# RWKV's LoRA products, key norm and first pair of heads moved between the layer's first weight fills, mixed tiles rounded one by one, and the feed-forward output's wait split by part

## The reference

```python
h = _rms(x) * norm1_g
proj = h @ w_in            # aq, ak, av | rw: r, k, v, wd, ad, gd | rq, rk, rv, rg | three gates
# RWKV-7 on rw: z = h + shift_mu * (h_prev - h), over 14 tiles of 128 columns
w_log = -softplus(-(w0 + tanh(wd) @ w2)) - 0.5 ; a = sigmoid(a0 + ad @ a2) ; g = sigmoid(gd) @ g2
kk = k * k_k ; kk = kk / max(norm over the head of kk, 1e-12) ; k = k * (1 + (a - 1) * k_a)
# then a scan over positions for 8 heads of 64 (here 4 pairs), bonus = sum(r * k * r_k) * v
mixed = g0 * (attention @ w_attn_o) + g1 * (rwkv @ w_rwkv_o) + g2 * (retention @ w_ret_o)
x = x + mixed @ w_out
h2 = _rms(x) * norm2_g
x = x + (silu(h2 @ w_ffn_gate) * (h2 @ w_ffn_up)) @ w_ffn_down
```

## Time and profile before

| | |
|---|---|
| time, median of 3 runs | 3206.34 us (3206.17 to 3213.61) |
| the profiled execution | 3204.21 us, of it 3202.4 us span |
| PE busy in the span | 97% |
| mean granted TensorE clock | 0.989 |
| DVE, ACT, POOL busy | 36%, 34%, 45% |

### The profile page before, as it was taken

How to read it: one execution, slowest core, us unless ns; L and a number is a source line. 1 busy time by engine, 2 the same in 40 slices (tenths; PEclk the granted TensorE clock), 3 DMA queues, 4 the chain that set the end, 5 groups by cost and what they waited for, 6 DMA issues and landing times.

```text
span 3202.4 us, 52487 instructions
## 1 busy us (share of the span) xinstructions
PE 3103.2 (97%) x20754; PEld 2474.5 (77%) x20754; DVE 1140.3 (36%) x1645; ACT 1100.8 (34%) x1547; POOL 1431.9 (45%) x1824
## 2 busy tenths in 40 slices
PE   8998989999999999999999999999999999899999
PEld 6887778868878777887777888787688877688877
DVE  3025532361110456232556322226533156542210
ACT  4444543342222433113443322222411245432222
POOL 3542244635555454223335555556322242565555
PEclk9999899999999999999999999999999999999999
DMA  5223332213223232114323222233221242422223
GB/s 219 98 99 119 119 113 82 96 53 105 98 92 105 79 108 99 61 61 161 110 89 139 97 93 98 94 110 118 82 77 62 100 159 73 151 99 94 96 98 125
DMA packets 102130, 330.89 MB, mean 103 GB/s; under 512 B 10064, under 2 KB 10448, under 8 KB 101200
## 3 DMA queue, kind: packets, MB, share of 16 engines
q1 hardware_dynamic: 75088, 272.87, 25.0%
q10 hardware_dynamic: 26880, 55.65, 4.8%
HBM read 299.64 MB, written 28.84 MB: 103 GB/s over the span
## 4 chain that ended last, share of the span: by engine, by line
issue 40%; POOL 31%; PE 25%; DVE 1%; DMA 1%; ACT 1%; POOLq 0%; DVEq 0%; SPq 0%; ACTq 0%
POOL w_lo L317 31%; PE psum L346 20%; PE psum L682 4%; DMA H<-scratch 0%; DMA arena<-in_w_ada 0%; DVEq L1507 0%; POOLq L313 0%; PE psum L878 0%; PE psum L899 0%; POOLq L323 0%; DVE HL L1510 0%; PE psum L901 0%; PE psum L858 0%; DVE arena L2100 0%; PE psum L895 0%
## 5 line engine op out<-in xcount | busy, mean ns | idle before, releaser
L317 POOL TENSOR_TENSOR w_lo<-w_raw,w_hi 128x256 fp32r<-128x256 f32 x1820 | 1431.7, 819 | 1766.2 <-ACT w_hi L932 1567.8
L346 PE MATMUL psum<-XH,w_hi 128*128 128x512 f32 x2592 | 1052.2, 406 | 9.6 <-DVE XL L1510 3.5
L346 PE MATMUL psum<-XH,w_lo 128*128 128x512 f32 x2592 | 1014.5, 391 | 0.0
L346 PE MATMUL psum<-XL,w_hi 128*128 128x512 f32 x2592 | 1014.2, 391 | 0.0
L932 ACT ACTIVATE w_hi<-w_raw 128x1024 fp32r<-128x1024 f32 x436 | 460.3, 1056 | 807.5 <-PE psum L346 699.5
L346 PEld LDWEIGHTS psum<-XH,w_hi 128*128 128x128 f32 x2592 | 489.0, 189 | 145.1 <-issue 27.0
L346 PEld LDWEIGHTS psum<-XL,w_hi 128*128 128x128 f32 x2592 | 488.8, 189 | 105.1
L346 PEld LDWEIGHTS psum<-XH,w_lo 128*128 128x128 f32 x2592 | 489.6, 189 | 101.1 <-issue 7.7
L346 PE MATMUL psum<-HH,w_hi 128*128 128x512 f32 x976 | 391.3, 401 | 27.6 <-DVE HL L1510 20.7
L346 PE MATMUL psum<-HL,w_hi 128*128 128x512 f32 x976 | 385.5, 395 | 0.0
L346 PE MATMUL psum<-HH,w_lo 128*128 128x512 f32 x976 | 385.4, 395 | 0.0
(11 more groups left out here) (328 smaller groups left out, 2378.3 us busy)
## 6 DMA issues: line engine op xcount, KB each, us to landing
w_raw<-in_fills SPq DMA_DIRECT2D x488, 512.0 KB, 3.2
scratch<-arena ACTq DMA_DIRECT2D x86, 256.0 KB, 2.0
arena<-scratch ACTq DMA_DIRECT2D x10, 1024.0 KB, 7.8
arena<-in_w_ada SPq DMA_DIRECT2D x4, 2048.0 KB, 19.4
H<-scratch ACTq DMA_DIRECT2D x4, 2048.0 KB, 14.9
scratch<-H SPq DMA_DIRECT2D x2, 2048.0 KB, 8.3
arena<-scratch ACTq DMA_DIRECT2D x2, 2048.0 KB, 9.0
arena<-scratch ACTq DMA_DIRECT2D x2, 1792.0 KB, 19.7
```

Of the source, the lines that this page charges most:

```text
L317: ins = nc.gpsimd.tensor_tensor(w_lo[:, to:to + FILL // 4], w_raw[:, of:of + FILL // 4], w_hi[:, to:to + FILL // 4].bitcast(F32), ALU.subt ...
L346: ins = mm(out_ap, wt[:, w:w + 128], xt[:, x0:x0 + T], start=first and k == 0 and o == 0, stop=last and k == n - 1 and o == 2)
```

## The change

In each hybrid layer:

- The z fills come in another order (`Z_ORDER`): the tiles of wd, ad and gd first, then k, r, the two attention tiles, v. SP loads them one by one in that order. They are `z_fill(q)`, written out, no longer a loop from q = 4 to 11.
- Of RWKV's preparation, the three groups of LoRA products stand behind z fills 5, 7 and 9, the sums of squares of k behind z fill 11 (PE). ACT evaluates and takes out accordingly, between its roundings of weights; it does the key norm's Ln and Exp ahead of rounding behind z fill 12. DVE does the running sum of pair 0 at z fill 9, its key (`key(0)`) at 12 and its operands (`operands(0)`) at 13, ahead of the subtractions into XL. The shift comes with its own fill.
- Between the first mid fill and the scan there are now four bonus products with 13 mid blocks behind each (60 blocks in PREP instead of 80); SCAN has 172 instead of 152, three at each of its steps, and 3 or 2 instead of 4 or 3 at its last six.
- Attention's and retention's outputs are rounded and subtracted tile by tile, two of them before ACT's and DVE's last work on retention, and `gemm512`'s first half fill waits tile by tile.
- Gate A is fetched before retention's output is rounded, and waited for alone; gate C comes next, H last, with a wait of its own.
- Each mixed tile is rounded as soon as it is summed, between the roundings of weights, and DVE subtracts the one before.
- `gemm2816` (all three layers) waits for the first 16 tiles at its first block and for the last six at its third part (blocks 17 to 22).

```diff
-R_KB, U_KB = 92, 44
+R_KB, U_KB = 94, (68, 70, 72, 74, 101, 103, 105, 107)
+
+Z_ORDER = [14, 15, 6, 7, 8, 9, 2, 3, 4, 5, 0, 1, 10, 11, 12, 13]
...
-PREP = [8, 8, 8, 6, 6] + 4 * [11]
-SCAN = [2 + k % 2 for k in range(SLOTS * NCH // 2)] + [4, 4, 4, 4, 3, 3]
+PREP = [8] + 4 * [13]
+SCAN = [3] * (SLOTS * NCH // 2) + [3, 3, 3, 3, 2, 2]
...
@@ -623,15 +630,41 @@
-                gemm_rms(f0, c0, 8, 24 * l, 2 * l, l)
+                gemm_rms(f0, c0, 0, 24 * l, 2 * l, l)
...
+                def z_fill(q):
+
+                    j = q % 4
+                    pe.wait_ge(lo_ready, f0 + q + 1)
+                    pe.wait_ge(chunk_out[j], c0 + q // 4 + l * SKEW[j])
...
+                        if q == 15 and k < DT - 1:
...
+
+                def lora(of, rows, x, out):
+
+                    for n in range(4):
+                        if out:
+                            pe.wait_ge(sem("rw_lev"), 12 * l + 4 * out - 4 + n + 1)
+                        mm(bank(4 + n), A(88, 128, of + 128 * n)[rows], A(x)[rows], start=True, stop=True).then_inc(sem("rw_lora"), 1)
+
+                for q in range(4, 16):
+                    z_fill(q)
+                    if q == 5:
+                        pe.wait_ge(sem("rw_act"), 2 * l + 1)
+                        pe.wait_ge(sem("lora_in"), 16 * l + 16)
+                        lora(0, slice(0, 64), 40, 0)
+                    elif q == 7:
+                        lora(0, slice(64, 128), 40, 1)
+                    elif q == 9:
+                        lora(512, slice(0, 128), 42, 2)
+                    elif q == 11:
+                        pe.wait_ge(sem("rw_act"), 2 * l + 2)
+                        for p in range(PAIRS):
+                            ins = mm(bank(4 + p), C("blk1", 128), rp("rn", T, p * T), start=True, stop=True)
+                        ins.then_inc(sem("rp_ss"), 1)
 
...
+                    mm(bank(4 + p), C("blk1", 128), rp("rk", T, (p + 1) % 2 * T), start=True, stop=True).then_inc(sem("rp_bn"), 1)
+                    fill(PREP[1 + p])
...
@@ -1252,19 +1264,60 @@
+                act.preload_act_table(ACT.Sigmoid)
...
+                z_hi = lambda q: hi(f0 + q // 4 * 4, q % 4)
+                act.wait_ge(sem("rw_mix"), 14 * l + 2)
+                fn(A(40)[0:64], A(40)[0:64], ACT.Tanh)
+                fn(A(42), A(42), ACT.Sigmoid).then_inc(sem("rw_act"), 1)
...
+                    for n in range(4):
+                        act.wait_ge(sem("rw_lora"), 12 * l + first + n + 1)
+                        bias = {"bias": P2(l, name, n)} if name else {}
+                        fn(A(kb, T, n * T), bank(4 + n), func, **bias).then_inc(sem("rw_lev"), 1)
...
+                z_hi(4)
+                z_hi(5)
+                lora_out(76, 0, ACT.Sigmoid, "w0")
+                z_hi(6)
+                z_hi(7)
+                lora_out(44, 4, ACT.Sigmoid, "a0")
+                z_hi(8)
+                z_hi(9)
+                ln_exp_tables()
+                lora_out(52, 8, ACT.Copy)
+                z_hi(10)
+                act.wait_ge(sem("rw_mix"), 14 * l + 6)
+                for p in range(PAIRS):
+                    ins = fn(rp("rn", T, p * T), A(24, T, p * T), ACT.Square, scale=P2(l, "k_k", p))
+                ins.then_inc(sem("rw_act"), 1)
+                decays(0)
+                z_hi(11)
+                act.wait_ge(sem("rp_mx"), l + 1)
+                fn(rp("rn", 4 * T), rp("rn", 4 * T), ACT.Ln)
+                nc.scalar.drain()
+                fn(rp("rn", 4 * T), rp("rn", 4 * T), ACT.Exp, scale=-0.5).then_inc(sem("rp_rn"), 1)
+                z_hi(12)
+                z_hi(13)
+                z_hi(14)
...
+                    fn(XH[:, t * T:(t + 1) * T], A(U_KB[t]), ACT.Copy).then_inc(sem("rms_hi"), 1)
+                z_hi(15)
...
                 dve.wait_ge(sem("rms_rstd"), 2 * l + 1)
                 for q in range(4):
                     take(q, q, f0 + q + 1)
+                    shift(Z_ORDER[q] - 2, q)
...
+                for q in range(4, 12):
+                    take(q, q % 4, f0 + q + 1)
+                    normed(q - 4)
+                    shift(Z_ORDER[q] - 2, q % 4)
+                    if q == 9:
+                        sums(0)
...
+                def key(p):
...
+                def operands(p):
...
+                dve.wait_ge(sem("rp_ss"), l + 1)
+                ts(rp("rn", 4 * T), bank(4, 4 * T), 1e-24, None, ALU.max).then_inc(sem("rp_mx"), 1)
+                for q in range(12, 15):
+                    take(q, q % 4, f0 + q + 1)
+                    shift(Z_ORDER[q] - 2, q % 4)
+                    if q == 12:
+                        key(0)
+                    elif q == 13:
+                        operands(0)
+                for t in range(DT):
+                    dve.wait_ge(sem("rms_hi"), 24 * l + 8 + t + 1)
+                    s = slice(t * T, (t + 1) * T)
+                    lo(XL[:, s], A(U_KB[t]), XH[:, s]).then_inc(sem("rms_x"), 1)
+                take(15, 3, f0 + 16)
+                shift(Z_ORDER[15] - 2, 3)
+
+                drain()
+                for p in range(1, PAIRS):
+                    sums(p)
+                    key(p)
+                    operands(p)
+                    bonus(p - 1)
                 bonus(PAIRS - 1)
...
-                entries(first, f0 + 16, ADA_LATER)
+                entries(first, f0, ADA_LATER)
+                for n, e in enumerate(Z_ORDER):
+                    sp.wait_ge(lo_ready, f0 + n - 1)
+                    sp.dma_start(w_raw[:, n % 2 * FILL:(n % 2 + 1) * FILL], dram["fills"][f0 + ADA_LATER + e])\
+                        .then_inc(w_loaded[n % 2], 16)
...
+
+            def gemm512(f, c, tile0, skew, fills=range(4), ready=None):
...
-                        blocks(j, HH, HL, bank(b), range(4 * h, 4 * h + 4), range(tile0, tile0 + 4), True, True)\
-                            .then_inc(fill_done if h else half_done, 1)
+                        blocks(j, HH, HL, bank(b), range(4 * h, 4 * h + 4), range(tile0, tile0 + 4), True, True,
+                               None if j or h else ready).then_inc(fill_done if h else half_done, 1)
...
-                        if j == 0:
-                            pe.wait_ge(sem("ffn_lo"), value)
+                        if part != 1:
+                            pe.wait_ge(sem("ffn_lo"), value - (FT - 16 if part == 0 else 0))
...
-                pe.wait_ge(sem("at_y"), 2 * l + 1)
-                gemm512(f0 + 64, c0 + 17, 0, l + 1)
-                pe.wait_ge(sem("at_y"), 2 * l + 2)
-                gemm512(f0 + 68, c0 + 19, 4, l + 1)
+                gemm512(f0 + 64, c0 + 17, 0, l + 1, ready=lambda k: pe.wait_ge(sem("at_y"), 8 * l + k + 1))
+                gemm512(f0 + 68, c0 + 19, 4, l + 1, ready=lambda k: pe.wait_ge(sem("at_y"), 8 * l + 4 + k + 1))
...
+                    if p == PAIRS - 1:
+                        mixed(0, at("q", T))
+                        mixed(1, at("q", T, T))
...
+                def mixed(t, y):
+
+                    fn(HH[:, t * T:(t + 1) * T], y, ACT.Copy).then_inc(sem("at_yh"), 1)
...
-                fn(HH[:, 0:4 * T], A(AT["q"], 4 * T), ACT.Copy).then_inc(sem("at_yh"), 1)
                 act.preload_act_table(ACT.Sigmoid)
                 act.wait_ge(sem("rt_done"), l * PAIRS + PAIRS)
                 for k in range(MID - 5, MID - 1):
                     act.wait_ge(spilled[k % 4], spill_done(l, k))
-                fn(HH[:, 4 * T:8 * T], A(RQ, 4 * T), ACT.Copy).then_inc(sem("at_yh"), 1)
-                from_scratch(A(76, 8 * T), GATE_A, 8, "gate_a_h_in")
-                from_scratch(H[:], H_TILE, 8, "gate_a_h_in")
+                from_scratch(A(76, 8 * T), GATE_A, 8, "gate_a_in")
+                for t in range(4):
+                    mixed(4 + t, A(RQ, T, t * T))
                 takes(ATT[PAIRS][0])
                 from_scratch(A(92, 7 * T), GATE_C, 7, "gate_c_in")
+                from_scratch(H[:], H_TILE, 8, "h_out_in")
                 gate = lambda kb, q: fn(A(kb, 2 * T, 2 * q * T), A(kb, 2 * T, 2 * q * T), ACT.Sigmoid).then_inc(sem("gate_s"), 1)
...
-                gemm512(f0 + 68)
                 for j in range(8):
                     act.wait_ge(sem("mix_sum"), 16 * l + 16 + j + 1)
                     fn(HH[:, MIX_HI[j] * T:(MIX_HI[j] + 1) * T], A(16, T, j * T), ACT.Copy).then_inc(sem("mix_hi"), 1)
+                    if j % 2 == 0:
+                        hi(f0 + 68, j // 2)
...
+                            if h0 == 8 and j:
+                                mix_low(j - 1)
+
+                def mix_low(j):
+
+                    dve.wait_ge(sem("mix_hi"), 8 * l + 8 + j + 1)
+                    h0, l0 = MIX_HI[j] * T, MIX_LO[j] * T
+                    lo(HL[:, l0:l0 + T], A(16, T, j * T), HH[:, h0:h0 + T]).then_inc(sem("mix_lo"), 1)
...
+                def low_part(t, y):
+
+                    dve.wait_ge(sem("at_yh"), 8 * l + t + 1)
+                    lo(HL[:, t * T:(t + 1) * T], y, HH[:, t * T:(t + 1) * T]).then_inc(sem("at_y"), 1)
...
```

(34 more changed lines are left out.)

121 lines of the change are left out of this document (21 added, 100 removed).

## The result

The changed kernel takes 3154.74 us (median of four runs, 3152.10 to 3155.77), the kernel before 3206.26 on the same chip (3203.7 to 3213.61). The ratio is 0.9834, with a 95% interval of 0.9817 to 0.9852. The forecast was 3158 us, with a range of 3147 to 3174. The profiled execution took 3155.64 us, with a span of 3153.9 us and a mean granted clock of 0.992 (forecast: near 0.994; before: 0.989). So the span is 48.5 us shorter.

The account below looks back on a forecast made before the run. PE, busy 97% of the span, bounds the kernel: gaps 36.6, XL trickle 5.8 and half-clock loss 17.0 make 59.4 us. Less 10.8 given back, 48.6 off 3204.2 gives 3155.6; plus 2.1 for the median, 3158; range 3147 to 3174.

Parts of the forecast that it names:

- The gaps of the layer's end: PE's waits at attention's output, `w_out`, feed-forward output (HL, 17.0 us) go; gate waits of 6.8 fall to 0.5 per layer.
- Feed-forward and mixed tiles at 0: Feed-forward output and mixed tiles: PE no longer waits, as the last tiles are ready before PE needs them; 0 left.
- Rival E: Split waits at mixed tiles and feed-forward do nothing because a later part is as late: 3176 us; chance 0.05.
- LoRA, activations, low weights, clock behind them: RWKV's preparation: waits for LoRA's activations (5.0 us) and low weights (3.5) go, with half-clock stretches of 6.8 and 10.2.
- Rival D: LoRA products between z fills lower the clock, eating the 48.6 us gain; 3222 with 16 us each; chance 0.04.
- The XL trickle: First mid fill: waits for XL tiles become one gap of about 2 us and a trickle, losing 3.2 us per layer.
- The 26.6 for DVE's start: DVE starts its eight subtractions into XL 26.6 us after fill 11 is done; undisturbed 25.8, at most 29.6.
- Rival B: DVE too slow beside POOL: XL tiles come at the upper bound, a 7.9 us loss per layer; 3172 us; chance 0.17.
- The clock behind it, 1.7: Behind the gap at the first mid fill, one half-clock stretch costs 1.7 us for the two layers together.
- The bonus slack falls 3.5, 2.5, 1.6, no wait: Bonus products before the scan: DVE needs 10.84 us per further pair, PE 9.8; slack shrinks but no wait remains.
- One halved stretch behind an untouched gap, 1.7: One half-clock stretch appears behind a gap the change doesn't touch, such as the two of 1.85 us; costs 1.7.
- The 20 blocks at nothing: Mid blocks moved from PREP to SCAN cost nothing; the scan is bound by PE's work, only 0.7 us could be covered.

## Why the prediction was right, point by point

- **The gaps of the layer's end** (HL 17.0, gates 6.8 down to 1.0): right in each place, each shown by its own experiment. The gates kept 0.55 and 0.20 us, the prediction had 0.5 each. (The 0.43 in the expectation above is another wait, that for L1331, 0.6 us in both layers, which the prediction didn't have.) Gate A took 10.2 us to land, it had 9.0 + 1.
- **Feed-forward and mixed tiles at 0**: right, neither waits any more. Rival E is refuted by the two experiments that undo them, 12.3 and 6.6 us.
- **LoRA, activations, low weights, clock behind them**: right. There is no wait and no half clock behind any of the groups. Rival D didn't come.
- **The XL trickle**: right in kind, one gap near 2 us (2.3) and a slow fill, but too small. The 26.6 for DVE's start was in part luck. Its lower bound, 25.8 "when undisturbed", used the 3.85 us of the earlier trace rows, in which two of the operations already ran beside POOL (1.18 and 1.23 us for 0.68). And the two strided operations aren't slow for their layout: L1966 took 0.68 us at 1182.49, where POOL was idle when it began, and 1.21 to 1.23 beside POOL in later pairs. Pair 0's operands took 7.1 us instead of 5.4, the take and shift behind them 2.3 instead of 2.95. DVE began the subtractions at 26.8 instead of 26.6, took 7.04 us for 6.6, and the first bonus product started at 35.0 instead of 34.0 (1196.70 less 1161.7). That makes a loss of 4.2 a layer for 3.2. Rival B's upper bound, 7.9, was not reached: POOL stands idle between its bursts, as assumed.
- **The clock behind it, 1.7**: wrong in mechanism. The halved stretch was there, in one layer, and cost nothing, since both layers took 32.0 us.
- **The bonus slack falls 3.5, 2.5, 1.6, no wait**: wrong by a little. DVE needed 12.3 and 11.4 us for a pair (its scans of pairs 1 to 3 begin at 1197.93, 1210.23 and 1221.61) where the earlier trace rows gave 10.84, and the last product of each layer waited 0.35, 0.7 us in both. A bonus product waiting for `rp_rk` was one of the prediction's own signs of being wrong. It came, with these 0.7 us.
- **One halved stretch behind an untouched gap, 1.7**: three stood there. The one at 1080.1 is followed by a wait for DVE (L428) which shrank from 3.5 to 1.9 us, so it cost nothing; the other two cost 1.7 each, 3.4.
- **The 20 blocks at nothing**: right, and a little better. Four waits of 0.3 in the scan went (1.1 us in all).

Recounted so, 8.4 (XL) + 0.8 (gates) + 0.6 (L1331) + 0.7 (bonus) + 3.4 (halved) = 13.9 were given back, for 10.8 predicted, less 1.1 in the scan: 59.4 - 13.9 + 1.1 = 46.6, and 48.5 went. The table of stages finds two amounts that aren't the change's. In the first hybrid layer, feed-forward out is 4.0 us shorter, of which the halved stretch is 1.7: in that stage of this one execution of the kernel before, products started every 0.2333 us, and in the same product of its other layers and of the changed kernel every 0.2289. Why is open. And the block ahead of the hybrid layers is 1.5 us shorter although a gap of 2.6 is closed in it: its other waits and halved stretches took 1.1 more. With + 2.3 and - 1.1 it is 47.8, and 0.7 is left unassigned.

That the forecast for the profiled execution (3155.6) is so close to its 3155.64 is thus in part offsetting errors, which is luck: 3.1 more given back than forecast, against 1.1 in the scan, 1.2 from those two amounts and the 0.7 left over. The 3158 lies 3 us above the measured median because 2.1 were added for the median, which this time was 0.9 below the profiled execution.

## What to carry to other kernels

Fill an engine's gaps by asking which producer is last there, and let each consumer wait for the piece that it needs next: the two lines at the feed-forward output gave 12.3 us, the whole rearrangement of the z fills 16.2 (17.5 by the stages of the traces). When a side engine's list becomes the bound, moving work within it only moves the wait; look for filler work of the main engine (here the mid blocks) that can push the deadline back, and first show that it is worth nothing where it is. Before adding up waits, see whether they stand in series: undoing one of these cost 14.2 us or 3.1, depending on what the others left. And read a change's worth stage by stage in the traces: here the sum of four medians hid by chance that the waits overlap.

## What the runs showed of the hardware

**A halved clock ahead of a wait is free.** In four of the fourteen profiled executions, the changed kernel's among them, the stretch at about 1080 us is halved, and in those four the wait of L428 is 1.9 us, in the other ten 3.5. The time from the end of the wait ahead of that stretch to the end of L428's is 14.65 or 14.66 us in all fourteen (1078.74 to 1093.40 in the changed kernel, 1080.20 to 1094.86 in the kernel before). Half clock is to be charged only where PE isn't waiting soon after.

**The same gap halves the clock in one execution and not in the next.** Over those fourteen, which are of variants of one kernel, the untouched gap of 1.85 us at RWKV's output had a halved stretch behind it 6 times in 28. The gap of 2.3 ahead of the first mid fill had one 10 times in 14, in seven executions; shortened to 1.72, none in 4. One gap's cost can't be forecast to better than these 1.7 us.

**DVE and POOL slow each other.** Durations in ns (min, median, max) of DVE's subtractions into XL, of POOL's beside them, and of POOL's in the scan:

```profile
L1540 DVE TENSOR_TENSOR XL<-arena,XH x8: 678/950/1225, 1188.5 to 1194.9; 128x512 fp32r<-128x512 f32 x8
...
L323 POOL TENSOR_TENSOR w_lo<-w_raw,w_hi x4: 978/1178/1190, 1188.8 to 1192.0; 128x256 fp32r<-128x256 f32 x4
...
L323 POOL TENSOR_TENSOR w_lo<-w_raw,w_hi x59: 724/738/750, 1299.8 to 1479.6; 128x256 fp32r<-128x256 f32 x59
```

POOL's burst ends at 1193.21, and DVE's subtractions, which start at 1188.52, go from 1.22 to 0.68 us there. I had expected DVE to be slowed; that POOL goes from 0.74 to 1.18 as well is new. The two together start anew every 1.14 us, where alone DVE starts every 0.60 and POOL every 0.69: they nearly take turns, and the price is shared by both. DVE's take, which reads PSUM (0.69 us at 1176.21), ran beside a subtraction of POOL that took 0.74, and neither was slowed. By the Trainium skill (SBUF — State Buffer, section "SBUF: two separate sides") a DVE operation with two SBUF inputs and a GpSimd one that reads SBUF exclude each other for a whole instruction. The trace agrees in which pairs are slowed and in the pace; it doesn't show the port.

**What differs between executions sits in few places.** Over the fourteen, the first product of the first block's feed-forward output starts between 937.4 and 943.2 us, with 13.9 to 19.0 us of waits for loaded weights ahead of it. From feed-forward in to feed-forward out a hybrid layer takes 240.3 us in all that have the split wait, to 0.05. So stages behind that block can be compared to half a microsecond once the halved stretches are counted, and the medians of four runs can't.
